# Experts' down weights in one run of four rows a partition, and the hidden product transposed by eight 64x64 identity matmuls

## The reference, cut to what matters

```python
for e in range(N_EXPERTS):                            # 32
    hid = jax.nn.silu(t @ w_gate[e]) * (t @ w_up[e])  # D = 1024 -> F = 512
    y = y + gates[:, e:e + 1] * (hid @ w_down[e]).astype(f32)   # F = 512 -> D = 1024
```

## Time and profile before

| | |
|---|---|
| runs | 1090.42 us median of 3 (1088.92 to 1090.57) |
| the profiled execution's own time | 1090.6 us |
| its span | 1088.8 us |
| TensorE busy | 1067.8 us, 98% |
| DVE, ACT, POOL busy | 550.8, 344.0, 289.8 us |
| moved by DMA | 263.39 MB |

### The profile page before, as it was taken

The page is one execution under the profiler, slowest core; times in us unless marked ns, Lnnn a source line. Parts: engine busy times, 40 slices in busy tenths (PEclk is TensorE's granted clock), DMA queues, the critical chain, the costliest instruction groups (busy, mean ns, idle before and its releaser), DMA issues.

```text
span 1088.8 us, 13007 instructions
## 1 busy us (share of the span) xinstructions
PE 1067.8 (98%) x5078; PEld 681.4 (63%) x5078; DVE 550.8 (51%) x1030; ACT 344.0 (32%) x620; POOL 289.8 (27%) x196
## 2 busy tenths in 40 slices
PE   7999999999999999999999999999999999998998
PEld 6777888777788888888888853333333333333333
DVE  5533895699850422339992453333444444442434
ACT  6356632445442554541233311111111111111111
POOL 6733344455551544443523110000000000000000
PEclk9999999999999999999999999999999999999999
DMA  8613333224151222254359989999999999999994
GB/s 214 161 40 78 78 78 78 62 74 116 30 143 39 65 74 58 60 186 126 94 217 370 343 352 402 424 426 424 424 423 426 426 425 423 424 426 425 426 420 199
DMA packets 125935, 263.39 MB, mean 242 GB/s; under 512 B 11953, under 2 KB 97969, under 8 KB 109489
## 3 DMA queue, kind: packets, MB, share of 16 engines
q1 hardware_dynamic: 122128, 255.75, 63.1%
q0 software_dynamic: 2352, 4.18, 1.1%
q10 hardware_dynamic: 1392, 2.62, 0.6%
HBM read 262.33 MB, written 4.20 MB: 245 GB/s over the span
## 4 chain that ended last, share of the span: by engine, by line
PE 96%; DMA 2%; issue 1%; ACT 1%; DVE 0%; SPq 0%; POOL 0%; ACTq 0%; POOLq 0%
PE bank L1138 21%; PE bank L685 19%; PE bank L704 14%; PE bank L1152 11%; PE bank L940 8%; PE bank L1031 4%; PE bank L1158 3%; PE bank L1159 3%; PE bank L912 2%; PE bank L895 2%; PE bank L1125 1%; PE bank L1144 1%; PE bank L903 1%; PE bank L780 1%; PE bank L842 1%
## 5 line engine op out<-in xcount | busy, mean ns | idle before, releaser
L2154 POOL TENSOR_TENSOR piece_r<-arena,piece_r 128x1024 fp32r<-128x1024 f32 x84 | 202.5, 2418 | 242.6 <-ACT piece_r L1294 242.3
L1138 PE MATMUL bank<-arena,work 128*64 128x512 f32 x1024 | 226.7, 595 | 1.2 <-issue 1.2
L685 PE MATMUL bank<-piece_r 128*128 128x512 f32 (+1 forms) x936 | 218.6, 389 | 0.0
L685 PEld LDWEIGHTS bank<-piece_r 128*128 128x128 f32 x936 | 172.5, 188 | 35.9 <-issue 3.5
L1138 PEld LDWEIGHTS bank<-arena,work 128*64 128x64 f32 x1024 | 72.9, 137 | 138.3 <-issue 138.3
L704 PE MATMUL bank<-piece_r 128*128 128x512 f32 x672 | 155.8, 391 | 0.5 <-ACT piece_r L1294 0.5
L704 PEld LDWEIGHTS bank<-piece_r 128*128 128x128 f32 x672 | 125.3, 188 | 29.2 <-issue 3.5
L2012 DVE TENSOR_TENSOR arena<-bank,arena 128x512 f32<-128x512 f32 x126 | 80.9, 685 | 103.5 <-PE bank L1159 103.1
L1294 ACT ACTIVATE piece_r<-arena 128x1024 fp32r<-128x1024 f32 x83 | 87.5, 1057 | 94.9 <-DMA arena<-w_branch_gla_in 49.4
L2268 POOL DMA_INDIRECT arena<-x_rows,idx_pair x15 | 15.2, 1011 | 330.2 <-PE bank L1125 314.5
L2037 DVE SCALAR_TENSOR_TENSOR bias<-bank,slot_sc,bias 128x256 f32<-128x256 f32 x32 | 15.5, 484 | 156.3 <-ACT bias L1537 156.3
(11 more groups left out here) (275 smaller groups left out, 1158.9 us busy)
## 6 DMA issues: line engine op xcount, KB each, us to landing
arena<-w_exp_gate_in SPq DMA_DIRECT2D x28, 2048.0 KB, 26.5
arena<-w_exp_up_in SPq DMA_DIRECT2D x27, 2048.0 KB, 22.4
arena<-w_exp_down_in SPq DMA_DIRECT2D x18, 2048.0 KB, 29.4
arena<-w_in_in SPq DMA_DIRECT2D x68, 512.0 KB, 4.5
wdn_spare<-w_exp_down_in SPq DMA_DIRECT2D x9, 2048.0 KB, 30.9
arena<-w_exp_up_in SPq DMA_DIRECT2D x8, 1024.0 KB, 10.4
arena<-w_exp_gate_in SPq DMA_DIRECT2D x6, 1024.0 KB, 23.2
arena<-w_exp_down_in SPq DMA_DIRECT2D x5, 1024.0 KB, 9.5
```

The source lines that it names most:

```text
L685: last = mm(bank[n % 2][:, cols], w[:, k, :], h[:, k, cols], start=(i == 0 and k == 0), stop=(i == 2 and k == K - 1))
L1138: last = mm(onto[hf * WIDE:(hf + 1) * WIDE, :], hTe[q][:, k, :], both[:, :, k, hf * HALF:(hf + 1) * HALF], start=(k == 0), stop=(k == K - 1))
L2154: Q.tensor_tensor(quarter(w_lo, q), quarter(w_raw, q), quarter(w_hi, q).bitcast(F32), ALU.subtract).then_inc(s["wlo_ready"], 1)
```

## The change

The down weights are laid out so that a partition holds four consecutive rows of an expert's matrix, 16 KB in one run, where it held two runs of 8 KB. `hid` must then be turned so that row 4q+j of half h lands on partition h*64+q: the columns 4q+j of the upper 64 partitions and of the lower 64 partitions are turned apart from each other, each by a product with a 64x64 identity, 4 values of j by 2 halves. Two transposes of 128x128 become eight products with 64 rows, 64 stationary columns and 64 moving columns. ACT's copy and the products of `down` read and write as many elements as before, under other names of the axes. In the overflow loop one further transpose is put ahead.

```diff
-    wdd = w_exp_down[0].rearrange("e (h p c) d -> e p h c d", h=2, c=2)
+    wdd = w_exp_down[0].rearrange("e (p h c) d -> e p h c d", h=2, c=2)
...
-        hidT = bias[3][:, 256:512].rearrange("p (c h s) -> p c h s", c=2, h=2)
+        hidT = bias[3][:, 256:512].rearrange("p (j s) -> p j s", j=F // P)
...
             def hidden_transposes(done):
-                for c in range(2):
-                    last = tr(bank[5][:, c * P:(c + 1) * P], hid.rearrange("p (q c) -> p c q", c=2)[:, c, :], ident[:, :])
+                for j in range(F // P):
+                    for hf in range(2):
+                        rows = slice(hf * WIDE, (hf + 1) * WIDE)
+                        last = mm(bank[5][rows, j * WIDE:(j + 1) * WIDE],
+                                  hid.rearrange("p (q j) -> p j q", j=F // P)[rows, j, :], ident[rows, rows],
+                                  start=True, stop=True)
                 last.then_inc(done, 1)
...
-                        last = mm(onto[half * WIDE:(half + 1) * WIDE, :], hidT[:, k % 2, k // 2, :],
+                        last = mm(onto[half * WIDE:(half + 1) * WIDE, :], hidT[:, k, :],
                                   halves[k // 2][:, k % 2, hf * 512:(hf + 1) * 512], start=(k == 0), stop=(k == F // P - 1))
...
                     pe.wait_ge(s["hid_ready"], t + (NE + 1))
+                    tr(bank[5][:, HALF:HALF + P], hid[:, 0:P], ident[:, :])
                     hidden_transposes(s["hidT_ps"])
...
-                A(hidT, bank[5][:, 0:HALF].rearrange("p (c h s) -> p c h s", c=2, h=2), ACT.Copy)\
+                A(hidT, bank[5][:, 0:HALF].rearrange("p (j s) -> p j s", j=F // P), ACT.Copy)\
                     .then_inc(s["hidT_ready"], 1)
```

## The result

The changed kernel takes 1108.15 us (median of 4 runs, 1107.98 to 1108.82) where the kernel before took 1090.29 in the same session: a ratio of 1.0165, 95% interval 1.0152 to 1.0177. It is 17.9 us slower. The forecast had said slower by 2.8 us, with a range up to 1098.5; the direction was right and the size far off. The profiled execution has a span of 1106.2 us against 1088.8.

The account below looks back on a forecast made before the run. TensorE sets the pace, except for 6.4 us waiting for weights in experts 24 to 28. 9.2 us added less 6.4 gives +2.8 on 1090.6, 1093.4; the runs' median lies 0.2 lower: 1093.2 us, range 1088.6 to 1098.5.

Parts of the forecast that it names:

- Added: Turning of `hid`: eight float32 products, 16 instructions per expert, 0.029 us apart, ending 0.15 us later than the old transposes.
- Products further than 0.03 apart: Sign that would prove the forecast wrong: the new stage's instructions spaced more than 0.03 us, where 0.029 was taken.
- no overlap of the two tiles: Upper bound for the new products: the two 64x64 tiles do not overlap, twice the spacing, 0.44 us more per expert.
- Rival C: Slower by much: the two 64x64 tiles do not overlap, 14 us more, time about 1107; chance 0.10.
- The hold at a change of tile shape: On TensorE, the next weight load starts only about 0.1 us after the last column has streamed.
- the way through the combine tile: Path from `hid` through L1158 and L1159 to `down`: 1.26 us against 0.98, so 0.28 us more per expert.
- The 6.4 us of waits: TensorE waiting for late weights in experts 24 to 28; added TensorE work before expert 28 first comes out of these.
- Rival D: The 6.4 us are not late weights, so all 9.2 us would be added: 1099.6 us; chance 0.05.
- The down loads: 27 loads of 2 MB in 16 KB runs: 1.3 us less DMA time, 1 to 3 possible; gain in the sum 0.
- The parts costed at nothing: ACT's copy, `down`'s reads, DVE and POOL work counted as equal; the overflow loop's added transpose does not run.
- Rivals A and B: A: faster, under 0.13 us an expert, about 1088, chance 0.08. B: no change, 0.15 to 0.26, middle 1090.6, chance 0.32.

Follow-up runs that it names:

- with neighbours: Changed kernel, but each 64x64 product takes 64 neighbouring columns of an unchanged `hid`, so the output differs: 1093.25 us, ratio 1.0025.
- interleaved products: Kernel before with the new down layout, its transposes kept, gate and up reading moving weights in 8-byte runs 16 bytes apart: 1094.84 us, ratio 1.0041.
- one tile with 16 bytes: Changed kernel, but all eight products of an expert go to the same 64x64 tile, columns 16 bytes apart: 1138.76 us, one run.
- packed write: Changed kernel, but VectorE writes `hid` so that the 64 columns of each product are neighbours: 1098.21 us, ratio 1.0071.

## Why the prediction was right or wrong

**The step that failed** is in "Added": "No row has just that. The nearest in size are L1006 and L1118 ... so I take 0.029." The rows were near in the number of columns but their stationary columns are neighbours in memory, and mine were 16 bytes apart. The price is 0.060. "Products further than 0.03 apart" was the prediction's own first sign of being wrong. It had no term for the distance at all: its bound above was "no overlap of the two tiles", a cause that isn't there. In the sum the stage's 16 instructions were thus 15 x 0.031 = 0.47 us too short, and 32 x 0.47 = 15.0 us are what is missing: 1093.2 + 15.0 = 1108.2, measured 1108.15. The trace of before held a sign of it: among transposes of one shape, the loads of L976 (neighbours) take 140 ns and those of L1144 (8 bytes apart) 198.

**Rival C** had the right time (about 1107) for the wrong reason. The range left it out at a chance of 0.10; a second cause of the same size, uncounted, was the one that came.

**The rest of the step held.** The hold at a change of tile shape, the order in which L1162, L1163 and L1156 follow, and that the way through the combine tile is the later one: with neighbours the chain came to 1.28 against 1.26, and the time to 1093.25 against the forecast 1093.2.

**The 6.4 us of waits** were what the prediction took them for. They are gone in after (0.04 us idle in 940 to 1060). The account "added time less 6.4" fits over a wide span: +2.8 measured for 32 x 0.30 - 6.4 = 3.2 with neighbours, +4.3 for 4.2 with interleaved products, +17.9 for 18.2 after, and for one tile with 16 bytes, where L1156 starts 2.72 behind `hid`, +48.1 for 32 x 1.74 - 6.4 = 49.3. It runs up to 1.4 us high in the runs with a packed write (32 x 0.48 - 6.4 = 9.0 for 7.6). Two things in the traces make up most of that. Expert 1 does not pay: its L1152 or L1156 starts 1.78 to 1.79 us behind the stage's start before, after and with the packed write alike, because TensorE waited 1.03 us for ACT there already. And the profiled execution with the packed write reached its first stage 0.69 us earlier than that of before (646.90 for 647.59). 31 x 0.48 - 6.4 - 0.69 = 7.8, for a span 7.5 us longer. The prediction, too, counted expert 1 in full (0.3 us with neighbours, 0.8 with the step), so it is in part luck that the sums above come out to 0.1 us. Rival D, that the waits stay, is out: with 0.77 us an expert it would have given +24.6.

**The down loads** were costed at 1.3 us, with 1 to 3 possible; alone they gave 2.0. That their gain is lost when TensorE is late held: with both parts or with the products alone the medians are 0.1 us apart, though the intervals of their ratios would hide up to 2 us. Loads of down weights issued in 940 to 1000 landed after 22.9 us in after, for 42.1.

**The parts costed at nothing** were nothing: L1549 takes 0.38 us, L1156 x16 3.65 as L1152 did, and L1125 still has 120 instructions, so the overflow loop did not run. Rivals A and B needed 0.13 and 0.15 to 0.26 us an expert and got 0.77; even with neighbours it is 0.30, with the hold at the exit in it.

The Trainium skill has the rule that was left unused: "Advanced Engine Details and Errata", Memory Cachelines, says that SBUF has lines of 16 bytes and needs at least two accesses to one line to run at full rate. The product runs here agree with it: 8 bytes apart, two columns to a line, 0.70 us for the stage; 16 bytes apart 1.18. The transposes do not follow it: their loads are slower at 8 bytes already (198 ns for 141), and no slower at 32 (193). The rule of the Trainium skill that the prediction did weigh, that row tiles can't use one PSUM bank together ("TensorEngine Tiling (Array Packing)", Restrictions and Gotchas), is not what slowed it: with neighbours two row tiles write bank 5, on different partitions, at 0.031 us an instruction.

What stays open is why a step of 32 bytes makes the load of a transpose about 0.05 us longer (193 ns for 140) and that of a product of 128 columns 0.14 (335 for L1087's 192); the runs do not say what differs inside. The exact distance at which products begin to pay lies above 8 and at or below 16 bytes; 12 was not tried.

## What to carry to other kernels

When a product's operand is a slice with a step, look for a row with the same step in bytes, not only the same shape; a float32 product whose stationary columns are 16 bytes or more apart pays twice for each weight load, while transposes of the same data, in a row of eight, lose next to nothing. Two transposes by themselves lose 0.06 us even at 8 bytes. Moving such a step elsewhere moved its price too: to VectorE (0.13 to 0.18 us), or to the moving operand (5% of the largest line). And where TensorE waits late for loads that fell behind, find how much it waits in all before costing either side: here the first 6.4 us of more work were free, and the faster loads were worth nothing once they were used.

## What the runs showed of the hardware that was not expected

- Weight loads of float32 products: 0.058 us for 64 columns that are neighbours, 0.119 at 16 bytes apart; 128 columns 0.111 as neighbours, 0.236 at 32 bytes apart.
- Weight loads of float32 transposes, 128 columns: 140 ns long as neighbours, 198 at 8 bytes apart, 193 at 32. In a row they start 0.109 us apart as neighbours and 0.111 to 0.113 at 32 bytes.
- Two 64x64 tiles that lie on different rows and different columns of the array overlap almost fully, also when both write one PSUM bank on different partitions: 0.031 us an instruction together, 0.058 with one tile; with the step 0.060 and 0.119.
- A moving operand in runs of 8 bytes, 16 bytes apart, streams 5% slower (7.42 us against 7.09 for L1138's 32).
- A VectorE instruction of 128x256 on two inputs takes 484 ns in order, 666 with its output scattered and 669 with its inputs read 16 bytes apart.
